# First block: selection rounds spread two to a projection tile and over the bias steps of attention units 0 to 19

## The chip, the cores and the metric

The kernel runs on one core of one Trainium2 chip. The metric is the device time of one execution in microseconds. Five engines work side by side, each with its own queue that is worked off strictly in order: PE (TensorE) multiplies, ACT (ScalarE) and DVE (VectorE) do elementwise work and empty PE's accumulators, POOL (GpSimd) adds a few tensors and issues DMAs, SP (SyncE) issues the weight loads. They meet only in semaphores: an instruction that finishes raises one, another engine's queue stands still until a count is reached.

## The reference, cut to what matters

Two model blocks run one after the other on 512 tokens of width 1024. The change lies in the first, which has two layers. Each layer is: SwiGLU feed-forward, RMS norm, one input projection to 2244 columns, three kinds of attention (8 heads with a sliding window, 4 heads in blocks, 4 heads with a learned selection of keys), output projection, SwiGLU again. The part that matters is the selection: for each query, the 128 best-scored keys are kept and all others are masked.

```python
dots = jnp.einsum('bqhd,bsd->bqhs', qi, k_idx).astype(jnp.float32) * (IDX_DIM ** -0.5)
score = jnp.einsum('bqhs,bqh->bqs', jax.nn.relu(dots), wi)
score = jnp.where((key_pos[None, :] <= tq[:, None])[None], score, -jnp.inf)
_, idx = lax.top_k(score, n_keep)        # n_keep = 512 // 4 = 128
...
s = jnp.einsum('bqhd,bqkd->bhqk', qc, k_sel).astype(jnp.float32) * scale + bias
```

The queries are handled in four blocks of 128. Block 0 has only 128 keys, so it needs no selection. Blocks 1, 2 and 3 have 256, 384 and 512 keys.

## The kernel before, in words

**Precision.** Each weight tile (128 x 1024) is split on its way: ACT copies `w_raw` into `w_hi` (line 167), DVE subtracts to get `w_lo` (line 174), and PE forms three products for each pair (lines 196 to 198). Three split tiles and three raw tiles are held at a time. ACT may split tile n + 3 only when PE has used tile n; DVE's `split_lo` of that tile waits for ACT's half.

**Projection (lines 1329 to 1352 for PE).** The 18 tiles of the input projection are worked in a fixed order. Tiles 0 to 3 give the selection's queries, its keys and the latent. Behind tile 3 PE forms the index scores and DVE adds them up in `work` (1152 columns: 256, 384 and 512 for the query blocks 1, 2, 3; the profile calls it `topk`). Tiles 4, 5 and 6 are the value trio: PE works them as one step, and only at its end are their three slots free. Tiles 7 to 17 are single again.

**Selection rounds (`topk_rounds`, from line 1147).** One call of `rounds(dve)` issues one round on DVE: `max` finds the eight largest values of each row (MAX8, line 1160), `match_replace` strikes them out (MATCH_VALUE_LOAD and MATCH_REPLACE8, line 1162). Sixteen rounds find 128 keys, so there are 48 rounds in a layer: 0 to 15 on 256 columns, 16 to 31 on 384, 32 to 47 on 512. The last round of each sixteen is followed by a comparison that turns the row into a mask (TENSOR_SCALAR, line 1166) and raises `sel_done`. In DVE's queue, four rounds stand behind the `split_lo` of each projection tile from tile 6 on. These are 12 tiles, so all 48 rounds stand in the queue before the attention starts; a loop behind the tiles issues whatever is left over, which is nothing.

**Attention (`Attention`, from line 521).** There are 64 units: four query blocks of 16 heads. Unit u is scored by PE (line 588), DVE adds the bias and takes the row maximum (`bias(u)`, line 720, the bias step), ACT takes the exponential (line 662), PE turns the probabilities (line 612), ACT or DVE copies them out (lines 689 and 764, DVE for odd units of the first block), PE multiplies by the values (line 627). DVE's queue holds, for each u: the copy of unit u if odd, then `bias(u + 2)`, then at the end of each eight units the division (lines 741 to 751). PE scores unit u + 2 only behind the turning of unit u. Before the first unit DVE clears `q_wide` (line 758), ACT fills it with the first queries (line 677), and only then can PE score unit 0. After each sixteen units the output of one query block is turned, the first time behind the turning of unit 17: PE line 597, ACT line 698, DVE line 775; ACT reaches that step behind the exponential of unit 19, and PE takes up unit 18 again when DVE is through with it. Before each bias step DVE calls `combined(eng, u)`, which for the selecting heads (units 28 to 31, 44 to 47 and 60 to 63) waits until POOL has added mask and bias.

Of the kernel before, what the change touches and what calls it, by code (L numbers as in the profile page):

```python
# [53 lines left out]
def program(nc, io):  # L54
# [11 lines left out]
    with top:  # L66
# [988 lines left out]
        def first_layers(ctx, shared, Hh, Hl, near, far, lv, upc, nsink, tri, QA, KD, VA, QB, KB, VB, QC, CKV, KCc, VC,  # L1055
# [43 lines left out]
            IDX_AFTER, CKV_AFTER, TRIO = 3, 8, 4  # L1099
# [47 lines left out]
            def topk_rounds():  # L1147

                state = {"n": 0, "sem": 3}

                def one(dve):
                    n = state["n"]
                    if n >= 3 * TOPK_ROUNDS:
                        return False
                    qb, r = n // TOPK_ROUNDS + 1, n % TOPK_ROUNDS
                    a, e = spans[qb]
                    dve.wait_ge(topk, state["sem"])
                    dve.max(best[:, :], work[:, a:e]).then_inc(topk, 1)  # L1160
                    dve.wait_ge(topk, state["sem"] + 1)
                    dve.match_replace(work[:, a:e], best[:, :], work[:, a:e], -3e38).then_inc(topk, 1)
                    state["sem"] += 2
                    if r == TOPK_ROUNDS - 1:
                        dve.wait_ge(topk, state["sem"])
                        dve.tensor_scalar(work[:, a:e], work[:, a:e], -2e38, BIG, ALU.is_gt, ALU.mult
                                          ).then_inc(sel_done, 1)
                    state["n"] += 1
                    return True

                return one
# [31 lines left out]
            with nc.Fori(0, DEPTH) as layer:  # L1203
                mlp_a.beside, mlp_b.beside = conditioning_beside(0, layer), conditioning_beside(1, layer)
                with nc.Block() as block:
                    @block.sync
                    def _(sp):
                        sp.dma_start(lv[:], io["layer_vecs"][bass.ds(layer, 1)].rearrange("a p n -> (a p) n")
                                     ).then_inc(vecs_in, 16)
                        st.load(sp, layer * LAYER1_TILES)  # L1210
# [156 lines left out]
                    def _(act):  # L1367
# [15 lines left out]
                        for j, (kind, dst) in enumerate(order):  # L1383
# [25 lines left out]
                            if j == IDX_AFTER:  # L1409
                                for i, (qb, _) in enumerate((q, i) for q in range(1, NQ) for i in range(4)):  # L1410
                                    nk = 128 * (qb + 1)
                                    act.wait_ge(idx_mm, i + 1)
                                    if i >= 2:
                                        act.wait_ge(acc_done, i - 1)
                                    act.activation(relu[:, i % 2, 0:nk], ps[:, 4 + i % 2, 0:nk], ACT.Relu, scale=1.0 / 16
                                                   ).then_inc(relu_done, 1)
# [20 lines left out]
                    @block.vector  # L1437
                    def _(dve):
                        st.start(st.split_lo, dve)
                        dve.wait_ge(vecs_in, 16)  # L1440
                        dve.tensor_scalar(nsink[:, :], lv[:, 25:33], -1.0, None, ALU.mult).then_inc(nsink_done, 1)
                        norms[0].vector(dve)
                        mlp_a.vector(dve)
                        dve.wait_ge(small, 64)
                        norms[1].vector(dve)
                        rounds = topk_rounds()
                        for j in range(N_IN1):
                            st.split_lo(dve, n_mix + j + st.n_hl)
                            if j == IDX_AFTER:

                                n = 0
                                for qb in range(1, NQ):
                                    a, e = spans[qb]
                                    for i in range(4):
                                        dve.wait_ge(relu_done, n + 1)
                                        w = WI[:, qb, i:i + 1]
                                        if i == 0:
                                            m = dve.tensor_scalar(work[:, a:e], relu[:, n % 2, 0:e - a], w, None, ALU.mult)
                                        else:
                                            dve.wait_ge(acc_done, n)  # L1460
                                            m = dve.scalar_tensor_tensor(out=work[:, a:e], in0=relu[:, n % 2, 0:e - a],
                                                                         scalar=w, in1=work[:, a:e], op0=ALU.mult,
                                                                         op1=ALU.add)
                                        m.then_inc(acc_done, 1)
                                        n += 1
                                    dve.wait_ge(acc_done, n)
                                    dve.tensor_tensor(work[:, e - 128:e], work[:, e - 128:e], tri[:, :], ALU.add
                                                      ).then_inc(topk, 1)
                            if j >= TRIO + 2:
                                for _ in range(4):  # L1470
                                    rounds(dve)
                            if j == CKV_AFTER + 1:
                                dve.wait_ge(ckv_inv, 1)
                                dve.scalar_tensor_tensor(out=CKV[:, :], in0=CKV[:, :], scalar=lv[:, 24:25], in1=relu[:, 0, :],
                                                         op0=ALU.mult, op1=ALU.mult).then_inc(ckv_n, 1)
                        while rounds(dve):
                            pass

                        def combined(eng, u):
                            if u == 0:  # L1480
                                eng.wait_ge(nsink_done, 1)
                            if u in comb_of:
                                eng.wait_ge(comb_done, comb_of[u] + 1)

                        att.vector(dve, combined)
                        proj.vector(dve)
                        norms[2].vector(dve)
                        mlp_b.vector(dve)
# [685 lines left out]
```

## Time and profile before

| | |
|---|---|
| median of 3 runs | 4356.09 us (4355.25 to 4361.63) |
| profiled execution | 4354.72 us, its span 4353.2 us |
| busy share PE, weight load, DVE, ACT | 91%, 74%, 52%, 36% |
| mean granted TensorE clock | 0.953 |

The span is what the profile covers; the execution's own time is 1.5 us more. The first block's layer 0 has its projection and attention between some 440 and 685 us, layer 1 the same about 1075.4 us later. Busy shares are means over the whole kernel. For this change the stretch between 500 and 612 us matters, and there the order of events on DVE, ACT and PE.

### The profile page before, as it was taken

How to read it: one execution, taken by the hardware profiler on the slowest of the kernel's cores; microseconds unless marked ns; L12 is line 12 of the kernel's file. 1: busy time of each engine (PE TensorE's matmuls, PEld its weight loads, DVE VectorE, ACT ScalarE, POOL GpSimd, SP SyncE). 2: the span in 40 equal slices, each digit the busy share in tenths (PEclk: the TensorE clock that was granted, in tenths of full speed). 3: DMA queues.
4: the chain of work that ended last, by engine and by line, in shares of the span. 5: the costliest groups of instructions: out<-in, count | busy, mean ns of one | idle time of the engine just before them, and what ended most of it. 6: DMA issues, size and time to landing. Idle time of an engine off the chain costs nothing. (4 is left out here: it accounts for less than half of the span.)

```text
span 4353.2 us, 52924 instructions
## 1 busy us (share of the span) xinstructions
PE 3941.1 (91%) x19258; PEld 3213.4 (74%) x19258; DVE 2270.2 (52%) x4044; ACT 1586.7 (36%) x2672; POOL 126.5 (3%) x188
## 2 busy tenths in 40 slices
PE   5999978999899997999969999699998679798999
PEld 3887766888688776688848887588887457576887
DVE  3665563666566666366632454355555344444555
ACT  2223353222322336322255454322221574743222
POOL 1000000000100000000000000000000000000000
PEclk9999989999999998999989999899999889899999
DMA  6443202443544220244211110121221110102332
GB/s 239 135 136 100 63 25 78 136 130 111 186 131 140 82 73 15 87 136 144 88 57 53 44 42 24 48 63 59 62 63 49 30 39 1 39 1 73 97 96 77
DMA packets 99854, 354.04 MB, mean 81 GB/s; under 512 B 11139, under 2 KB 14723, under 8 KB 98776
## 3 DMA queue, kind: packets, MB, share of 16 engines
q1 hardware_dynamic: 76632, 274.64, 20.8%
q0 software_dynamic: 18304, 70.33, 5.0%
q10 hardware_dynamic: 4736, 6.62, 0.4%
q8 instruction: 117, 1.92, 0.2%
q14 instruction: 65, 0.53, 0.0%
HBM read 345.73 MB, written 11.06 MB: 82 GB/s over the span
## 5 line engine op out<-in xcount | busy, mean ns | idle before, releaser
L167 ACT ACTIVATE w_hi<-w_raw 128x1024 fp32r<-128x1024 f32 x500 | 529.4, 1060 | 1902.5 <-PE ps L198 1733.9
L174 DVE TENSOR_TENSOR w_lo<-w_raw,w_hi 128x1024 fp32r<-128x1024 f32 x500 | 615.0, 1231 | 1161.2 <-ACT w_hi L167 1160.8
L196 PE MATMUL ps<-h_hi,w_hi 128*128 128x512 f32 (+1 forms) x2824 | 1094.2, 387 | 66.6 <-DVE h_lo L255 34.2
L197 PE MATMUL ps<-h_lo,w_hi 128*128 128x512 f32 (+1 forms) x2824 | 1083.3, 384 | 0.0
L198 PE MATMUL ps<-h_hi,w_lo 128*128 128x512 f32 (+1 forms) x2824 | 1082.1, 383 | 0.0
L196 PEld LDWEIGHTS ps<-h_hi,w_hi 128*128 128x128 f32 x2824 | 537.2, 190 | 192.3 <-issue 54.9
L198 PEld LDWEIGHTS ps<-h_hi,w_lo 128*128 128x128 f32 x2824 | 537.8, 190 | 103.9
L197 PEld LDWEIGHTS ps<-h_lo,w_hi 128*128 128x128 f32 x2824 | 538.8, 191 | 100.4 <-issue 1.4
L196 PE MATMUL ps<-a_hi,w_hi 128*128 128x512 f32 x1472 | 549.0, 373 | 3.3 <-DVE ctx_x L454 3.3
L197 PE MATMUL ps<-a_lo,w_hi 128*128 128x512 f32 x1472 | 546.8, 371 | 0.0
L198 PE MATMUL ps<-a_hi,w_lo 128*128 128x512 f32 x1472 | 546.0, 371 | 0.0
L196 PEld LDWEIGHTS ps<-a_hi,w_hi 128*128 128x128 f32 x1472 | 277.0, 188 | 57.2 <-DVE ctx_x L454 6.3
L198 PEld LDWEIGHTS ps<-a_hi,w_lo 128*128 128x128 f32 x1472 | 276.8, 188 | 49.1
L197 PEld LDWEIGHTS ps<-a_lo,w_hi 128*128 128x128 f32 x1472 | 277.1, 188 | 47.6
L454 DVE SCALAR_TENSOR_TENSOR x<-ps,x 128x512 f32<-128x512 f32 x352 | 231.5, 685 | 54.6 <-PE ps L198 52.6
L454 DVE SCALAR_TENSOR_TENSOR x<-ps,mod,x 128x512 f32<-128x512 f32 x256 | 188.0, 748 | 94.0 <-PE ps L198 94.0
L402 ACT ACTIVATE a_hi<-val 128x512 fp32r<-128x512 f32 (+1 forms) x184 | 106.0, 592 | 307.2 <-DVE val L438 307.2
L662 ACT ACTIVATE arena<-arena,nm 128x768 f32<-128x768 f32 (+3 forms) x160 | 130.9, 818 | 218.0 <-DVE nm L720 217.4
L240 PE MATMUL ps<-scratch,ones 128*128 128x512 f32 (+1 forms) x144 | 76.2, 682 | 98.8 <-ACT scratch L220 98.8
L612 PE MATMUL ps<-ident,arena 128*128 128x128 f32 x784 | 119.2, 284 | 31.7 <-DVE h_lo L775 26.4
L419 DVE TENSOR_TENSOR a_lo<-val,a_hi 128x512 fp32r<-128x512 f32 (+1 forms) x184 | 115.2, 640 | 62.5 <-ACT a_hi L402 62.5
L240 PEld LDWEIGHTS ps<-scratch,ones 128*128 128x128 f32 x144 | 27.3, 223 | 144.8 <-ACT scratch L220 124.2
(243 smaller groups left out, 4661.9 us busy)
## 6 DMA issues: line engine op xcount, KB each, us to landing
w_raw<-in_w_first SPq DMA_DIRECT2D x316, 512.0 KB, 3.6
w_raw<-in_w_mlp SPq DMA_DIRECT2D x128, 512.0 KB, 3.6
shared<-in_w_ada POOLq DMA_DIRECT2D x96, 512.0 KB, 4.3
w_raw<-in_w_odd SPq DMA_DIRECT2D x30, 512.0 KB, 3.6
w_raw<-in_w_even SPq DMA_DIRECT2D x26, 512.0 KB, 3.6
near_stage<-near_bias POOLq DMA_DIRECT2D x32, 256.0 KB, 2.9
bias_rows<-bias_line SPq DMA_DIRECT2D x1, 5120.0 KB
shared<-silu_cond POOLq DMA_DIRECT2D x4, 1024.0 KB, 4.9
```

What stands on the lines that cost most here:

```text
L167: act.activation(self.hi[:, n % H, :], self.raw[:, n % R, :], ACT.Copy).then_inc(self.hi_done, 1)
L174: dve.tensor_tensor(self.lo[:, n % self.n_hl, :], self.raw[:, n % self.n_raw, :], self.hi[:, n % self.n_hl, :].bitcast(F32), ALU.subtract) ...
L196: pe.matmul(out, lhs[0], rhs[0], start=start, stop=False)
L197: pe.matmul(out, lhs[0], rhs[1], start=False, stop=False)
L198: return pe.matmul(out, lhs[1], rhs[0], start=False, stop=stop)
L240: pe.matmul(self.acc(), ones[:, :], self.tmp["sq"][:, c % 2, 0:self.n], start=(c == 0), stop=(c == self.nk - 1)).then_inc(self.sum_done, 1)
L402: m = act.activation(self.hi[s][:, 2 * (c % 2) + j, :], self.val[s][:, j, :], ACT.Copy)
L419: m = dve.tensor_tensor(self.lo[s][:, a, :], self.val[s][:, j, :], self.hi[s][:, a, :].bitcast(F32), ALU.subtract)
L454: m = dve.scalar_tensor_tensor(out=stream["x"][:, o, :], in0=ps[:, self.down_bank(8 * c + o, s), 0:stream["n"]], scalar=self.gains(s, o), ...
L612: m = pe.transpose(ps[:, 4 + t % 2, 128 * j:128 * j + 128], tmp["s"][:, u % 2, 128 * (b + j):128 * (b + j) + 128], ident[:, :])
L662: act.activation(tmp["s"][:, u % 2, 0:n], tmp["s"][:, u % 2, 0:n], ACT.Exp, bias=tmp["nm"][:, u % 16:u % 16 + 1], scale=-1.0, accum_out=tm ...
```

## The change

DVE's queue now holds two rounds behind each projection tile from tile 4 (`TRIO`) on, in place of four from tile 6 on. The loop that issues what is left is gone. Instead `combined(eng, u)`, which DVE's queue passes before the bias step of each unit, issues one round as long as there are any. Fourteen tiles by two rounds are rounds 0 to 27; rounds 28 to 47 stand before the bias steps of units 0 to 19. No instruction is added or removed.

```diff
-                            if j >= TRIO + 2:
-                                for _ in range(4):
+                            if j >= TRIO:
+                                for _ in range(2):
                                     rounds(dve)
...
-                        while rounds(dve):
-                            pass
-
                         def combined(eng, u):
                             if u == 0:
                                 eng.wait_ge(nsink_done, 1)
+                            rounds(eng)
                             if u in comb_of:
                                 eng.wait_ge(comb_done, comb_of[u] + 1)
```

## Rows read from the trace of the kernel before

**Rows 1.** Busy time by stretch: PE, PEld, DVE, ACT, POOL; clock, DMA share, GB/s

```profile
500.00:563.50 63.50, 62.82 (x276) 51.12 (x276) 58.72 (x135) 24.22 (x33) 2.79 (x2) 1.00 0.33 100
563.50:579.60 16.10, 0.00 (x0) 0.01 (x1) 15.01 (x29) 1.80 (x4) 0.00 (x0) 0.64 0.22 65
579.60:600.00 20.40, 18.04 (x96) 14.63 (x97) 11.01 (x54) 16.88 (x68) 0.00 (x0) 0.87 0.01 2
```

**Rows 2.** Timeline of PE behind the projection (start us, us, ..., [idle before <-releaser])

```profile
579.63 1.19 PE L588 MATMUL ps<-shared,q_wide 128*128 128x128 f32 x4 [16.37 <-ACT q_wide L677]
```

**Rows 3.** Timeline of ACT at the projection's end, layer 0, then layer 1

```profile
563.35 1.06 ACT L167 ACTIVATE w_hi<-w_raw 128x1024 fp32r<-128x1024 f32 x1 [3.90 <-PE ps L198]
...
579.17 1.30 ACT L677 ACTIVATE q_wide<-shared 64x128 f32<-64x128 f32 x4 [14.28 <-DVE q_wide L758]
...
1638.74 1.06 ACT L167 ACTIVATE w_hi<-w_raw 128x1024 fp32r<-128x1024 f32 x1 [3.90 <-PE ps L198]
```

**Rows 4.** Timeline of DVE: one selection round on 384 columns to the next

```profile
525.88 0.55 DVE L1160 MAX8 best<-topk 128x8 f32<-128x384 f32 x1
...
527.11 0.56 DVE L1160 MAX8 best<-topk 128x8 f32<-128x384 f32 x1
```

**Rows 5.** Timeline of DVE: rounds on 512 columns and what follows them

```profile
549.40 0.36 DVE L1166 TENSOR_SCALAR topk<-topk 128x384 f32<-128x384 f32 x1
549.68 1.22 DVE L174 TENSOR_TENSOR w_lo<-w_raw,w_hi 128x1024 fp32r<-128x1024 f32 x1
550.82 0.69 DVE L1160 MAX8 best<-topk 128x8 f32<-128x512 f32 x1
...
551.62 0.68 DVE L1162 MATCH_REPLACE8 topk<-best,topk 128x512 f32<-128x512 f32 x1
552.33 0.69 DVE L1160 MAX8 best<-topk 128x8 f32<-128x512 f32 x1
...
556.17 0.68 DVE L1162 MATCH_REPLACE8 topk<-best,topk 128x512 f32<-128x512 f32 x1
556.76 1.22 DVE L174 TENSOR_TENSOR w_lo<-w_raw,w_hi 128x1024 fp32r<-128x1024 f32 x1
...
578.59 0.48 DVE L758 MEMSET q_wide<- 128x512 f32 x1
```

**Rows 6.** Timeline of DVE: bias steps of units 0, 1, 3; copy for unit 3

```profile
580.54 0.35 DVE L720 CUSTOM_DVE_ANT_0 scratch<-ps,bias_a,minus_sinks 128x128 f32<-128x128 f32 x1 [1.46 <-PE ps L588]
...
580.86 0.35 DVE L720 CUSTOM_DVE_ANT_0 scratch<-ps,bias_a,minus_sinks 128x128 f32<-128x128 f32 x1
...
583.06 0.35 DVE L720 CUSTOM_DVE_ANT_0 scratch<-ps,bias_a,minus_sinks 128x128 f32<-128x128 f32 x1
...
584.93 0.29 DVE L764 COPY scratch<-ps 128x128 f32<-128x128 f32 x1 [0.17 <-PE ps L612]
```

**Rows 7.** Timeline of DVE: bias steps of units 19, 20, 22, 24

```profile
599.82 0.47 DVE L720 CUSTOM_DVE_ANT_0 scratch<-ps,bias_a,minus_sinks 128x256 f32<-128x256 f32 x1
...
604.81 0.49 DVE L720 CUSTOM_DVE_ANT_0 scratch<-ps,bias_a,minus_sinks 128x256 f32<-128x256 f32 x1 [1.03 <-PE ps L588]
...
608.13 0.48 DVE L720 CUSTOM_DVE_ANT_0 scratch<-ps,bias_a,minus_sinks 128x256 f32<-128x256 f32 x1 [1.54 <-PE ps L588]
...
610.65 0.42 DVE L720 CUSTOM_DVE_ANT_0 scratch<-ps,bias_bc 128x256 f32<-128x256 f32 x1 [0.35 <-PE ps L588]
```

**Rows 8.** Timeline of DVE: zeroing and the step of unit 19 in layer 1

```profile
1653.97 0.48 DVE L758 MEMSET q_wide<- 128x512 f32 x1
...
1675.11 0.47 DVE L720 CUSTOM_DVE_ANT_0 scratch<-ps,bias_a,minus_sinks 128x256 f32<-128x256 f32 x1
```

**Rows 9.** Busy time by stretch: the granted clock behind unit 19

```profile
606.00:608.00 2.00, 2.00 (x11) 1.82 (x9) 0.49 (x2) 1.43 (x5) 0.00 (x0) 0.50 0.00 0
...
610.00:612.00 2.00, 2.00 (x15) 1.61 (x14) 1.17 (x7) 1.79 (x6) 0.00 (x0) 1.00 0.00 0
```

**Rows 10.** Waits between 480 and 780 us (total, times, longest)

```profile
DVE scratch L720 <- PE ps L588: 27.8, 39, 1.5
```

## The prediction

> **What bounds the kernel now.** I read the busy time by stretch first, then the timelines of PE, ACT and DVE where one stretch goes over into the next, then the waits.
>
> In the projection PE is the bound: it is busy for 62.82 of 63.5 us at full clock. DVE is nearly full as well, 58.72 us [rows 1]. The reader is to see what comes next: from 563.5 to 579.6 PE does nothing, while DVE works for 15.0 of 16.1 us [rows 1]. PE's timeline says 16.37 us idle, released by ACT's filling of `q_wide` [rows 2], and ACT had itself waited 14.28 us for DVE's zeroing of it [rows 3]. That zeroing stands in DVE's queue behind all 48 rounds, at 578.59 [rows 5]. So here the selection rounds set the end.
>
> Then units 0 to 19. Between 579.6 and 600.0 DVE is busy for 11.01 of 20.40 us, ACT for 16.88 [rows 1]. No engine is full. The units go round PE, DVE, ACT and PE, and DVE's waits are for PE's scores (27.8 us in 39 waits between 480 and 780 us [rows 10]). DVE has 9.4 us of gaps here.
>
> The change moves 20 rounds from a place where DVE alone sets the end into this second stretch. It is won if the gaps hold them. They don't.
>
> **The price of one round.** On 384 columns, MAX8 to the next MAX8 takes 527.11 - 525.88 = 1.23 us [rows 4]. On 512 columns it takes 552.33 - 550.82 = 1.51 us [rows 5]. Both include the wait of the next MAX8 for the replacement it reads. An instruction that doesn't read it starts sooner: the replacement at 551.62 is followed by a MAX8 0.71 us later, the one at 556.17 by a `w_lo` 0.59 us later [rows 5]. In the new order a bias step or a copy follows each round, neither of which reads `work`. I therefore take 1.23 - 0.12 = 1.11 and 1.51 - 0.12 = 1.39 us, and keep the full prices as the upper end. A comparison costs 549.68 - 549.40 = 0.28 us [rows 5], and must wait for its round, which then costs the full price.
>
> **Projection tiles 4 to 17.** Two rounds on 256 or 384 columns (at most 2.5 us) and a `w_lo` of 1.14 us (549.68 to 550.82 [rows 5]) make 3.6 us. PE's pace is 62.82 us for 11 tiles and a few small products, some 5.4 us a tile (x276 matmuls, 11 x 24 and 12 [rows 1]), so DVE stays ahead and PE waits for nothing new. Cost nothing. The rounds now put behind tiles 4 and 5 don't run under the value trio: each stands behind a `w_lo` whose `w_hi` needs the trio's slots. They run right behind the trio, ahead of the `w_lo` of tiles 8 and 9. The one for tile 8 comes 2 us later than now, with 5.4 us in hand.
>
> **The start of the attention, removed.** Tile 17 has two rounds behind it, numbers 26 and 27. They stand behind a `w_lo` whose `w_hi` ACT begins at 563.35, when PE has used tile 17, and needs 1.06 us for, to 564.41 [rows 3]. DVE: 564.45, plus 1.14 for `w_lo`, plus 1.23 + 1.11 for the rounds, is 567.93. There the zeroing starts. It started at 578.59 [rows 5]: 10.7 us sooner. In layer 1, ACT's start is at 1638.74 [rows 3] and the zeroing at 1653.97 [rows 8], which gives 10.65. Of PE's 16.4 us some 5.7 stay.
>
> **Units 0 to 19, added.** I sum DVE's work from the start of the zeroing to the start of unit 19's bias step, because with it DVE has no gap left. Before, this took 599.82 - 578.59 = 21.23 us [rows 5, 7], in layer 1 21.14 [rows 8].
> - Old work: zeroing 0.48, and 11.01 less the 0.18 that lies behind 599.82: 11.31.
> - Rounds 28 to 31: 4 x 1.11 = 4.44. Rounds 32 to 47: 16 x 1.39 = 22.24.
> - Two of them are followed by a comparison: 2 x (0.12 + 0.28) = 0.80.
> - Idle before unit 0: its bias step follows the start of the zeroing by 580.54 - 578.59 = 1.95 us [rows 5, 6], since ACT and PE come between. Zeroing and round 28 fill 1.59 of it: 0.36.
>
> The sum is 39.15 us, 17.9 more than now. Is it DVE at every unit? Two bias steps now lie at least 2 x 1.39 plus their own 2 x 0.3 apart, 3.4 us. PE and ACT need for the same way 3.32 us at their slowest, on 256 keys and at the low clock (unit 20 to 22: 608.13 - 604.81 [rows 7]; clock 0.50 [rows 9]); on 128 keys it is less. The copy for unit 3 came 584.93 - 583.06 = 1.87 us behind its bias step [rows 6]; the new order has 0.32 + 1.39 + 0.3 = 2.0 us there. So DVE sets it, if narrowly in places.
>
> **Behind unit 19.** ACT's exponential of unit 19, the turn (602.11) and unit 20 (604.81) hang on unit 19's bias step [rows 7], and are carried along. Nothing queued behind DVE has slack to give: PE's next score waits for the bias step two units earlier. POOL's additions need the first mask only at unit 28 and the last at unit 60; all are early enough. The weight tiles for the output projection are split before unit 0, as now. Net: 17.9 - 10.7 = 7.2 us a layer.
>
> **TensorE's clock.** Before, the clock is at 0.50 of full (1.2 GHz) between 606 and 608, behind the pause of the turn, and back at 1.00 from 610 [rows 9]. In the new order PE is idle for about half of each unit, so it will mostly be at the lower level before the turn as well, where DVE covers it. Then unit 20 starts at the lower level from its first instruction. I add 0.3 us a layer for that, nearly the price of one unit at the lower level instead of the higher (0.4, rival 2); the ends are 0 and 2.4 (six units).
>
> The Trainium skill ("TensorE: Matmul & The Clock Gate", section "Why this matters for your kernels") says that idle gaps between bursts of matmuls put the engine back to half rate. By that rule the trace agrees: 0.50 behind the turn [rows 9]. Taken as a rule for all of the sparse units and what follows them, it is the second rival.
>
> **Sum.** 7.2 + 0.3 = 7.5 us a layer, 15.0 for two. On the profiled execution, 4354.72 us with a span of 4353.2, that is 4369.7. The median of the runs lies 1.4 us above it, so the forecast is **4371 us**, slower by 0.35%. Ends a layer: if each bias step overlaps a further 0.08 us of the MAX8 behind it (as `w_lo`, 1.22 us long, is followed after 1.14 [rows 5]), 5.6; if no round overlaps its successor, 7.2 + 18 x 0.12 = 9.4, plus 2.4 for the clock, 11.8. That is 4367 to 4380.
>
> **Rivals.**
> 1. *The gaps hold the rounds (faster).* The rounds run while DVE waits for scores, units keep their pace, and only the earlier start is left: -10.7 x 2, 4334.7 us. For it: DVE is idle 46% of the stretch. It decides from the point where 20 rounds fit in the gaps. They are 27.5 us, the gaps 9.4 [rows 1], and a round of 1.39 us is longer than the single gaps (1.46 before unit 0 [rows 6] is the longest of the bias steps). Chance 0.04. The Trainium skill ("Perfetto Trace Analysis", section "Optimization Strategy") says that performance may be improved by interleaving stretches that have different bounds; taken alone it speaks for this rival. The rows say that DVE was already interleaved with PE in the projection (58.72 of 63.5 us), and that the change leaves some 1.8 of 5.4 us a tile idle there.
> 2. *The clock stays low behind unit 19.* Two units take 3.32 us at 0.50 and 2.52 at the higher level (unit 22 to 24 [rows 7]), 0.4 us a unit. If units 20 to 31 all run low, 12 x 0.4 = 4.8 us a layer, 4381 us. Against it: from unit 20 on PE's work is as dense as before, and there the clock was back at 1.00 from 610 on [rows 9]. Chance 0.09.
> 3. *The delay is given back later.* DVE's waits for scores behind unit 19 could shrink. Then the time is that of before, 4356 us. Against it: these waits are a ring through PE and ACT, started by unit 19 itself. Chance 0.05.
>
> My own case has 0.82.
>
> **How the numbers follow.** Some 0.2% (9 us) is what a measurement of this kernel can tell from no change. Slower by more: most of my case, 0.80, and rival 2: 0.89. Within: rival 3 and the low edge of my case: 0.07. Faster: 0.04. The range of 8 in 10 takes my case's ends, the spread of the medians, and half of rival 2: 4363 to 4381.
>
> **What would show it.** In the new profile, layer 0: the zeroing at about 568 and PE's idle time before unit 0 near 6 us; DVE busy for over 95% between there and unit 19's bias step, with MAX8 to bias step 1.4 us; that bias step at 607 (now 599.82); unit 20 behind it by 5.0 to 5.3 us; all later events 7 to 8 us later. Wrong if bias steps wait for PE's scores between units 4 and 19 (then PE or ACT sets the pace, and more time is lost), if PE waits for `w_lo` in tiles 8 to 17, or if the distance from unit 19 to the output projection changes.

## The result, and the profile after

The changed kernel takes 4367.49 us (median of 17 runs, 4356.48 to 4375.97), the kernel before 4355.81 us (17 runs, 4346.47 to 4366.00). The ratio is 1.0028, with a 95% interval of 1.0019 to 1.0036: slower by 12 us (8 to 16). The forecast was 4371 us, slower by 15, with a range of 4363 to 4381. The profiled execution took 4370.76 us with a span of 4369.2.

The rows that answer to those of before, by stretch (columns as in [rows 1]). The two stretches are the projection, and the way from the zeroing to unit 19's bias step:

```profile
500.00:563.50 63.50, 62.29 (x275) 50.64 (x273) 40.25 (x91) 24.22 (x33) 1.43 (x2) 1.00 0.37 108
567.10:604.50 37.40, 29.57 (x104) 23.51 (x104) 36.20 (x116) 17.79 (x69) 0.00 (x0) 0.51 0.02 8
```

DVE, busy for 58.72 us in the projection before, is now busy for 40.25, and PE works on as it did. Behind it DVE is busy for 36.20 of 37.40 us, where it was for 11.01 of 20.40 [rows 1]. So 18.5 us of DVE's work left a stretch in which PE set the pace and the rounds cost nothing, and went into one in which DVE sets it. Of the 20 rounds that moved, only the last 8 had run behind PE's last tile, where they were in the way. In the second stretch PE is busy for 29.57 of 37.4 us, at a mean clock of 0.51, and is held back by DVE.

PE, then ACT, behind the projection ([rows 2, 3] answer):

```profile
568.16 1.20 PE L588 MATMUL ps<-shared,q_wide 128*128 128x128 f32 x4 [5.88 <-ACT q_wide L677]
...
562.38 1.06 ACT L167 ACTIVATE w_hi<-w_raw 128x1024 fp32r<-128x1024 f32 x1 [3.90 <-PE ps L198]
...
567.71 1.31 ACT L677 ACTIVATE q_wide<-shared 64x128 f32<-64x128 f32 x4 [3.79 <-DVE q_wide L758]
...
1644.31 1.06 ACT L167 ACTIVATE w_hi<-w_raw 128x1024 fp32r<-128x1024 f32 x1 [3.90 <-PE ps L198]
```

PE's idle time went from 16.37 to 5.88 us: the gain.

DVE, from the zeroing on ([rows 5 to 8] answer). Rounds on 384 columns, then rounds on 512, with the bias step or copy that follows; the turn; layer 1:

```profile
567.13 0.48 DVE L758 MEMSET q_wide<- 128x512 f32 x1
567.53 0.50 DVE L1160 MAX8 best<-topk 128x8 f32<-128x384 f32 x1
...
568.97 0.35 DVE L720 CUSTOM_DVE_ANT_0 scratch<-ps,bias_a,minus_sinks 128x128 f32<-128x128 f32 x1 [0.28 <-PE ps L588]
569.25 0.08 DVE L720 DVE_READ_ACCUMULATOR2_ANT nm<- 128x1 f32 x1
569.25 0.56 DVE L1160 MAX8 best<-topk 128x8 f32<-128x384 f32 x1
...
570.37 0.34 DVE L720 CUSTOM_DVE_ANT_0 scratch<-ps,bias_a,minus_sinks 128x128 f32<-128x128 f32 x1
...
574.03 0.69 DVE L1160 MAX8 best<-topk 128x8 f32<-128x512 f32 x1
...
575.42 0.34 DVE L720 CUSTOM_DVE_ANT_0 scratch<-ps,bias_a,minus_sinks 128x128 f32<-128x128 f32 x1
575.69 0.08 DVE L720 DVE_READ_ACCUMULATOR2_ANT nm<- 128x1 f32 x1
575.69 0.29 DVE L764 COPY scratch<-ps 128x128 f32<-128x128 f32 x1
575.89 0.68 DVE L1160 MAX8 best<-topk 128x8 f32<-128x512 f32 x1
...
577.28 0.34 DVE L720 CUSTOM_DVE_ANT_0 scratch<-ps,bias_a,minus_sinks 128x128 f32<-128x128 f32 x1
...
602.33 0.41 DVE L764 COPY scratch<-ps 128x256 f32<-128x256 f32 x1
...
604.51 0.48 DVE L720 CUSTOM_DVE_ANT_0 scratch<-ps,bias_a,minus_sinks 128x256 f32<-128x256 f32 x1
...
606.80 1.68 DVE L775 TENSOR_TENSOR h_lo<-ps,h_hi 128x128 fp32r<-128x128 f32 x8 [1.81 <-ACT h_hi L698]
610.18 0.48 DVE L720 CUSTOM_DVE_ANT_0 scratch<-ps,bias_a,minus_sinks 128x256 f32<-128x256 f32 x1 [1.70 <-PE ps L588]
...
616.45 0.42 DVE L720 CUSTOM_DVE_ANT_0 scratch<-ps,bias_bc 128x256 f32<-128x256 f32 x1 [0.36 <-PE ps L588]
...
1649.05 0.48 DVE L758 MEMSET q_wide<- 128x512 f32 x1
...
1686.42 0.48 DVE L720 CUSTOM_DVE_ANT_0 scratch<-ps,bias_a,minus_sinks 128x256 f32<-128x256 f32 x1
...
1698.42 0.42 DVE L720 CUSTOM_DVE_ANT_0 scratch<-ps,bias_bc 128x256 f32<-128x256 f32 x1 [0.35 <-PE ps L588]
```

The reader is to see that after 568.97 no row has idle time in brackets until 606.80. From there to unit 19 DVE never waits for another engine: bias step to bias step is 1.40 us with a round on 384 columns (568.97 to 570.37) and 1.86 with one on 512 and a copy (575.42 to 577.28), where it was 1.0 on the mean before (580.54 to 599.82 for units 0 to 19 [rows 6, 7]). That is the loss: unit 19's bias step comes 37.4 us behind the zeroing, not 21.2.

### The profile page after: what moved, and what is told of

It reads as the page before. It is cut to its first block and busy times, and to the rows that moved or that the text cites. A ratio compares the mean times of both kernels' runs of the same rounds, so it can differ in the third digit from the quotient of the medians.

```text
span 4369.2 us, 52924 instructions
## 1 busy us (share of the span) xinstructions
PE 3968.1 (91%) x19258; PEld 3235.0 (74%) x19258; DVE 2263.0 (52%) x4044; ACT 1588.6 (36%) x2672; POOL 123.9 (3%) x188
```

## The experiments

Each was profiled; where a ratio stands, it is to the kernel before on the same chip. "Way A" is from the start of ACT's last `w_hi` of the projection to unit 19's bias step, "way B" from there to unit 24's. Before, they were 36.5 and 36.4 us, and 10.8 and 10.8 (layers 0 and 1) [rows 3, 7, 8]; changed, 42.1 and 42.1, and 11.9 and 12.0.

**The tiles' part alone.** Against the kernel before, whose loop behind tile 17 stays and now issues the last 20 rounds:

```diff
-                            if j >= TRIO + 2:
-                                for _ in range(4):
+                            if j >= TRIO:
+                                for _ in range(2):
                                     rounds(dve)
```

> One part of the change alone: two rounds per tile from the value trio on, but the last 20 rounds stand as one block behind tile 17, ahead of the zeroing of q_wide, and none at the bias steps. My account (DVE's queue alone sets the pace, and the gaps between bias steps take a third of the 20 rounds): the zeroing in layer 0 at 567.1 + 4 x 1.25 + 16 x 1.51 + 0.5 = 596.8 us, unit 19's bias step 21.2 us behind it at 618 (604.5 in the changed kernel, 599.8 before). Some 12.4 us a layer over the changed kernel, 18 over the kernel before: about 4392 us. Rival (the rounds hurt because they stand inside the ring of PE, ACT and DVE and lengthen it): with the ring free of them the time comes out at or below the changed kernel's 4367.

Measured: 4395.66 us, ratio 1.0085 (1.0070 to 1.0101), 37 us over the kernel before. DVE in this kernel:

```profile
598.98 0.48 DVE L758 MEMSET q_wide<- 128x512 f32 x1
...
620.20 0.47 DVE L720 CUSTOM_DVE_ANT_0 scratch<-ps,bias_a,minus_sinks 128x256 f32<-128x256 f32 x1
```

The zeroing comes 34.7 us behind the last `w_hi` (564.24), unit 19 follows it by 21.2 as before. So the gaps between the bias steps did hold part of what they were given: with the 20 rounds as one block, way A is 56.0 us, with the rounds spread over the units 42.1. The rival falls. Interleaving is worth 13.9 us a layer against the block. But in the kernel before only 8 of these 20 rounds were left behind the last tile; the other 12 ran beside PE's projection and cost nothing.

**Four per tile, twenty at the units.**

```diff
-                            if j >= TRIO:
-                                for _ in range(2):
+                            if TRIO + 2 <= j < TRIO + 9:
+                                for _ in range(4):
                                     rounds(dve)
```

> The units' part as in the changed kernel (rounds 28 to 47 at units 0 to 19), but the 28 rounds of the tiles are packed four to a tile on tiles 6 to 12, so none stands behind tile 17. My account: only the start changes. Behind tile 17 DVE has w_lo alone, so the zeroing comes 2.5 us sooner than in the changed kernel, at about 564.7 to 565.6 in layer 0, and everything behind it up to the end is 2.4 to 2.5 us a layer sooner: 4367.5 - 5 = 4362.5 us, still slower than before by some 7. Rival (how the rounds are spread over the tiles is what costs or helps, for instance by PE waiting for w_lo): PE shows new waits in tiles 8 to 12 and the 5 us are not seen.

Measured: ratio 1.0008 (0.9999 to 1.0018), against 1.0028 for the change.

```profile
565.54 0.48 DVE L758 MEMSET q_wide<- 128x512 f32 x1
...
602.60 0.48 DVE L720 CUSTOM_DVE_ANT_0 scratch<-ps,bias_a,minus_sinks 128x256 f32<-128x256 f32 x1
```

The zeroing stands 2.37 us behind the last `w_hi` (563.17), where it is 4.75 in the changed kernel, and way A is 39.4 in both layers: 2.7 us less, against 2.4 expected. PE shows no wait for `w_lo` in tiles 8 to 17, and from the first `w_hi` behind the trio to the last one it is 65.28 us in this run, in the changed kernel and in the one before. How the 28 rounds are spread over the tiles is of no account, except that two behind tile 17 stand on the path: 5 us of the 12 lost, by the timeline (the two intervals all but meet).

**Three per tile, six at the units.**

```diff
-                                for _ in range(2):
+                                for _ in range(3):
```

> The changed kernel with three rounds behind each tile from the value trio on, so that 42 stand in the tiles and only 6 at the units, 0 to 5. A test of the sum at another dose. My account: the zeroing of q_wide now has three rounds on 512 columns behind tile 17, 1.14 + 3 x 1.51 = 5.7 us behind ACT's w_hi, and DVE is up to 0.7 us late by then: some 570.5 in layer 0 where the last w_hi starts at 563.3. Units 0 to 5 then take 10.6 us from the zeroing to unit 5's bias step where the kernel before takes 6.7 (five steps of 1.39 + 0.3, three copies of 0.2, unit 0 hidden): 3.9 more. From unit 6 on the old pace. Net -8.0 + 3.9 = -4.1 us a layer under the kernel before, plus up to 1.1 for the clock behind the turn: ratio 0.998 to 0.9986, about 4348 to 4350 us where the kernel before has 4356. Rival (any round at a bias step costs the units more than DVE's own time): slower than before.

Measured: 4347.48 us against 4355.57, ratio 0.9982 (0.9972 to 0.9993): faster by 8 us.

```profile
569.60 0.48 DVE L758 MEMSET q_wide<- 128x512 f32 x1
...
580.61 0.34 DVE L720 CUSTOM_DVE_ANT_0 scratch<-ps,bias_a,minus_sinks 128x128 f32<-128x128 f32 x1
...
595.79 0.47 DVE L720 CUSTOM_DVE_ANT_0 scratch<-ps,bias_a,minus_sinks 128x256 f32<-128x256 f32 x1
```

Zeroing 7.05 us behind the last `w_hi` (7.2 expected), unit 5 at 11.0 behind that (10.6 expected), then 15.2 to unit 19, where it was 14.6 before. In that last stretch the mean clock is 0.78, and was 1.00 before; that this is what costs the 0.6 us isn't shown. Ways A and B together are 3.2 and 3.1 us shorter than before, 3.0 to 4.1 expected. The sum holds at another dose, and with the sign changed: the same change with a 3 for a 2 is a gain.

**PE's idle time in the units filled.**

```diff
+                    if self.fill and 1 <= u <= self.fill:
+                        pe.matmul(ps[:, 1, 0:256], ident[:, :], X[:, 0, 0:256], start=True, stop=True)
...
+            att.fill = 17
```

> The changed kernel, with one more matmul on PE (identity by 256 columns of x, into an accumulator bank that nothing reads) behind each of units 1 to 17 of the first block, so that PE's idle time in the units with rounds is filled. The result is unchanged. My account: the clock in units 0 to 19 covers nothing that counts, since DVE sets the pace there. Unit 19's bias step stays within 0.5 us of 604.5; if the clock goes up to 1.00 before the turn, the way from unit 19's bias step to unit 24's, 11.9 us in the changed kernel and 10.8 before, shrinks to about 10.8: 1.1 us a layer, 2.2 in all, 4365 us. If the clock stays at 0.50 in spite of the fill, nothing changes or it is slower by a few us. Rival (the low clock is the main cost of the change): with the clock up, unit 19's bias step comes several us sooner and the kernel comes to 4356 to 4360 us.

Measured: ratio 1.0030 (1.0019 to 1.0040), no different from the change. The clock from unit 6 to unit 10, first of the changed kernel, then of this one:

```profile
578.00:588.00 10.00, 8.13 (x30) 6.53 (x30) 9.73 (x33) 5.08 (x22) 0.00 (x0) 0.50 0.01 2
```

```profile
578.00:588.00 10.00, 8.45 (x41) 5.21 (x40) 9.72 (x33) 5.24 (x22) 0.00 (x0) 1.00 0.01 2
```

The clock went from 0.50 to 1.00 there (1.2 to 2.4 GHz), and DVE's order in time is the same to a hundredth: zeroing to unit 19's bias step 37.39 us, 37.38 in the changed kernel. So the low clock inside the units costs nothing. But way B stayed at 12.0: half of my expectation was wrong. PE's pause at the turn was 4.71 us, with the clock at 1.00 before it, and still PE took up unit 18 at the lower one (its two transposes take 0.66 us at the lower level and 0.41 at the higher):

```profile
608.79 0.66 PE L613 MATMUL ps<-ident,scratch 128*128 128x128 f32 x2 [4.71 <-DVE h_lo L778]
```

**The turn filled too.** On top of the last:

```diff
                         turn(self.turn_at[u - 1])
+                        if self.fill and u - 1 < 20:
+                            for _ in range(4):
+                                pe.matmul(ps[:, 1, :], ident[:, :], X[:, 0, :], start=True, stop=True)
```

> The changed kernel with PE's idle time filled as in the run with one more matmul behind each unit, and with four more matmuls (identity by 512 columns of x, some 0.86 us each, result unread) on PE behind the first turn of each layer, so that PE's pause between the turn's transposes and its next unit, 4.1 us in the changed kernel, 4.7 with the fill and 2.9 before, becomes one of some 1 us. The result is unchanged. My account: the pause is what puts PE at the lower clock when it takes up unit 18 again. Then the first transposes behind the turn take 0.41 us in place of 0.66, and the way from unit 19's bias step to unit 24's is 10.8 us in both layers in place of 12.0; unit 19's bias step itself stays 42.1 us behind the last w_hi. Ratio to the kernel before some 1.0025. Rival (the lower clock behind the turn has another cause, or is chance): 0.66 us and 12.0 us in one layer or both.

Measured: ratio 1.0023 (1.0009 to 1.0037). PE at the turn, in the changed kernel and in this one:

```profile
602.84 1.66 PE L597 MATMUL ps<-ident,scratch 128*128 128x128 f32 x8
...
608.62 0.66 PE L612 MATMUL ps<-ident,scratch 128*128 128x128 f32 x2 [4.12 <-DVE h_lo L775]
```

```profile
604.25 0.41 PE L613 MATMUL ps<-ident,scratch 128*128 128x128 f32 x2 [1.28 <-DVE h_lo L781]
```

Way A is 42.1 in both layers. The first transposes take 0.41 us in place of 0.66, and way B is 9.5 us in both layers, 2.4 less than changed and 1.3 less than before: more than expected, because the clock is now at 1.00 all the way (600.1 to 609.7). So with the units filled, PE's pause at the turn is what makes way B long. The 5 us of two layers don't show in the time: the ratio can't be told from the change's 1.0028.

In the changed kernel itself the clock shows the same, by stretch (columns as in [rows 1]), inside the pause:

```profile
604.50:607.50 3.00, 0.00 (x1) 0.00 (x0) 1.19 (x7) 2.37 (x11) 0.00 (x0) 1.00 0.00 0
607.50:608.60 1.10, 0.00 (x0) 0.01 (x1) 0.98 (x5) 0.00 (x0) 0.00 (x0) 0.50 0.00 0
```

After 37 us mostly at 0.50 it stands at 1.00 when PE stops, and falls to 0.50 while PE stands still, before unit 18. No run fills the turn and leaves the units sparse; that this alone would do is not shown.

**Both kernels profiled once more.**

> The kernel before, profiled once more: how much do the two numbers that I compare move by themselves? The start of the last w_hi of the projection in layer 0 was 563.35 before, 562.38 in the changed kernel and 562.5 to 564.2 in the runs derived from it. The way from unit 19's bias step to unit 24's was 10.83 and 10.83 before, 11.94 and 12.00 changed. If the clock's phase is by chance, one of the two layers may now show 11.5 to 12; if the sparse units cause it, both stay at 10.8.

> The changed kernel, profiled once more. From the last w_hi of the projection to unit 19's bias step 42.1 us in both layers, since DVE alone sets it (within 0.2). The way from unit 19's bias step to unit 24's again 11.9 to 12.0 in both layers if PE's longer pause at the turn makes it, 10.8 in one of them if it is chance.

Measured: 4350.03 us for the kernel before and 4370.71 for the changed one, one execution each. DVE of the kernel before, layer 1, and its PE behind the turn:

```profile
1672.34 0.47 DVE L720 CUSTOM_DVE_ANT_0 scratch<-ps,bias_a,minus_sinks 128x256 f32<-128x256 f32 x1
...
1684.61 0.42 DVE L720 CUSTOM_DVE_ANT_0 scratch<-ps,bias_bc 128x256 f32<-128x256 f32 x1 [0.36 <-PE ps L588]
...
1676.46 0.66 PE L612 MATMUL ps<-ident,scratch 128*128 128x128 f32 x2 [2.86 <-DVE h_lo L775]
```

Way B was 10.85 us in layer 0 and 12.27 in layer 1; the changed kernel had 11.97 and 12.20. Way A of the changed kernel was 42.1 in both layers again. That of the kernel before was 36.85 and 37.42, where the first profile had 36.47 and 36.37: without the rounds DVE doesn't set the pace alone, and the way is not fixed. So the change costs 6.4 and 4.6 us a layer between these two profiles, 6.8 and 6.9 between the first two. The last `w_hi` of layer 0 started at 562.52 and 562.68, so the 0.97 us between the first two profiles there is scatter. Counting the first turn of each layer in all profiles here without added matmuls on PE: where the pause is 2.86 us, PE's first two transposes take 0.41 us seven times and 0.66 five times; where it is 3.85 us or more (this order of rounds, and the run with four per tile), 0.66 in all six. Way B is 10.8 to 10.9 us in the seven, 11.1 to 12.3 in the five and 11.65 to 12.2 in the six. The change makes way B surely long, where it was so by chance; on the mean of the four layers of each kernel that is 12.0 against 11.2 us.

**All rounds in the projection.** DVE has 17.2 us of nothing to do under the value trio, in the kernel before:

```profile
499.15 1.23 DVE L174 TENSOR_TENSOR w_lo<-w_raw,w_hi 128x1024 fp32r<-128x1024 f32 x1 [17.24 <-ACT w_hi L167]
```

```diff
                         for j in range(N_IN1):
+                            if j == TRIO:
+                                for _ in range(TOPK_ROUNDS):
+                                    rounds(dve)
                             st.split_lo(dve, n_mix + j + st.n_hl)
...
-                            if j >= TRIO:
-                                for _ in range(2):
+                            if TRIO <= j < N_IN1 - 1:
+                                for _ in range(3 if j < 10 else 2):
                                     rounds(dve)
...
-                            rounds(eng)
```

> All 48 rounds inside the projection: the 16 rounds on 256 columns stand ahead of the w_lo of tile 7, so that DVE does them while PE works the value trio and DVE has 17.2 us of nothing to do; then three rounds behind each of tiles 4 to 9, two behind tiles 10 to 16, none behind tile 17 and none at the units. My account: 16 rounds of 0.98 us are 15.7 us and end before the trio does; the rest costs at most 3 x 1.51 + 1.14 = 5.7 us of DVE against PE's 5.4 a tile, mostly 4.2 to 4.9. So the zeroing comes at 564.5 + 1.1 = 565.6 in layer 0 (578.6 before, 567.1 changed) and the units run at their old pace, unit 19's bias step at 586.8. 13 us a layer under the kernel before: 4330 us. Rival (DVE beside the trio slows PE or ACT, or w_lo comes late for tiles 8 to 10): PE waits for w_lo, and less than half of the 26 us is seen.

Measured: 4333.43 us against 4358.6, ratio 0.9944 (0.9931 to 0.9958). By stretch (the trio, then tiles 7 to 17), and DVE:

```profile
482.00:500.00 18.00, 15.68 (x90) 15.36 (x88) 15.68 (x50) 3.88 (x10) 1.40 (x2) 0.99 0.00 1
500.00:563.50 63.50, 62.63 (x275) 51.05 (x276) 55.91 (x111) 23.78 (x32) 0.00 (x0) 1.00 0.36 105
```

```profile
566.37 0.48 DVE L758 MEMSET q_wide<- 128x512 f32 x1
568.10 0.35 DVE L720 CUSTOM_DVE_ANT_0 scratch<-ps,bias_a,minus_sinks 128x128 f32<-128x128 f32 x1 [1.25 <-PE ps L588]
...
588.31 0.47 DVE L720 CUSTOM_DVE_ANT_0 scratch<-ps,bias_a,minus_sinks 128x256 f32<-128x256 f32 x1
```

DVE was busy for 15.68 us under the trio, and PE shows no new wait for `w_lo`: it is busy for 62.63 of the next 63.5 us. The zeroing stands 2.4 us behind the last `w_hi` (15.2 before). By the ratio the gain was 24 us of 26 expected. Ways A and B together are 10.9 and 11.5 us shorter than before, 13 expected a layer; 1.2 of what is missing is way B, 12.0 in both layers. One cost was not expected: from the first `w_hi` behind the trio to the last it is 66.22 and 66.57 us in place of 65.28. In both layers PE waits here for DVE, which has rounds on 512 columns ahead of the latent's last step, `ckv`, before which PE can't start L1298:

```profile
529.24 1.12 PE L1298 MATMUL ps<-ckv,w_kv_up 128*128 128x512 f32 x2 [0.53 <-DVE ckv L1477]
```

In layer 0 PE takes 2.68 us from its last product ahead of L1298 to the next tile's first, in place of 1.90. So the rounds are not quite free there: 0.9 and 1.3 us.

**The zeroing ahead of the sixteen.**

```diff
                             if j == TRIO:
+                                dve.memset(q_wide[:, :, :], 0.0).then_inc(att.q_zero, 1)
```

> All 48 rounds in the projection as in the run that puts sixteen under the value trio, and the zeroing of q_wide moved ahead of those sixteen, so that ACT can fill q_wide as soon as it has emptied tile 17. My account: 0.48 us more under the trio, which fits barely or delays w_lo of tile 7 by nothing (1.2 us of room). ACT's filling of q_wide starts 1.2 us sooner (at 565.6 where the last w_hi starts at 564.0) and unit 0 with it: 1.2 us a layer, 2.4 in all, ratio to the kernel before 0.9938 where the other has 0.9944, about 4331 us. That is less than five rounds can tell; the timeline decides. Rival (ACT or the turn holds unit 0): no sooner than 4.1 us behind ACT's last w_hi.

Measured: 4326.65 us against 4355.57, ratio 0.9931 (0.9917 to 0.9945). ACT at the projection's end:

```profile
563.89 1.06 ACT L167 ACTIVATE w_hi<-w_raw 128x1024 fp32r<-128x1024 f32 x1 [3.90 <-PE ps L198]
564.85 0.58 ACT L1403 ACTIVATE shared<-ps 128x512 f32<-128x512 f32 x1
565.46 1.30 ACT L678 ACTIVATE q_wide<-shared 64x128 f32<-64x128 f32 x4
```

ACT goes from emptying tile 17 to `q_wide` with no wait. Unit 0's bias step follows the last `w_hi` by 2.6 us (4.1 in the run above, 17.2 before). 1.5 us in layer 0 and 1.7 in layer 1, 1.2 expected; the ratios alone can't tell the two runs apart.

**The same, with three turns filled.** Two matmuls of 512 columns on PE behind the turns at units 17, 33 and 49, nothing in the units.

```diff
                         turn(self.turn_at[u - 1])
+                        if self.fill and u < len(units):
+                            for _ in range(2):
+                                pe.matmul(ps[:, 1, :], ident[:, :], X[:, 0, :], start=True, stop=True)
```

> The version with all rounds in the projection and the early zeroing, and two matmuls more (identity by 512 columns of x, result unread) on PE behind the turns of units 17, 33 and 49 in each layer of the first block, so that PE's pause of 2.9 us at each turn becomes one of some 1.2 us. The result is unchanged. My account: PE takes up the next unit at the higher clock and keeps it, as in the run with the filled turn, where the way from unit 19's bias step to unit 24's fell to 9.5 us (10.8 to 12.0 without). That is 1.3 to 2.5 us a turn, six turns, 8 to 15 us: ratio to the kernel before 0.990 to 0.9915, about 4315 us. Rival (the gain in that run needs the longer fill or the filled units): 10.8 us or more at the turns, ratio 0.993 as without the fill.

Measured: 4317.99 us against 4360.31, ratio 0.9913 (0.9900 to 0.9927): the fastest of all. PE's pause is 1.15 us in place of 2.86 and its first transposes take 0.41 us at all six turns, where the run above had 0.66 at four of the six. Way B is 9.5 us in both layers (10.85 and 11.08 above). From turn to turn it takes PE 23.17 and 25.84 us in layer 0, in place of 24.65 and 27.37, and 23.16 and 25.83 in layer 1, in place of 24.71 and 28.38.

```profile
586.85 1.88 PE L647 MATMUL ps<-x,ident 128*128 128x512 f32 x4
589.88 0.41 PE L613 MATMUL ps<-ident,scratch 128*128 128x128 f32 x2 [1.15 <-DVE h_lo L780]
```

The intervals of this run and the one above overlap, so it is the timeline, 1.3 to 2.6 us for each of six turns, and not the ratios that shows what the fill is worth.

## Why the prediction was right

By its own steps, in us, for layer 0 and layer 1, from the first profile of each kernel:

| step | forecast | measured |
|---|---|---|
| last `w_hi` to zeroing | 4.58 | 4.75, 4.74 |
| zeroing to unit 19's bias step | 39.15 | 37.38, 37.37 |
| the 20 rounds and 2 comparisons in it | 27.48 | 27.6 |
| the rest of DVE's work in it, idle time included | 11.67 | 9.8 |
| unit 19 to unit 24 | 10.8 + 0.3 | 11.94, 12.00 |
| net over before, a layer | 7.5 | 6.8, 6.9 |

- *Projection at no cost.* Right: 65.28 us from the trio's end to the last `w_hi` before and after. The run with four per tile shows that PE is indifferent to how these 28 rounds lie there.
- *The start.* Right to 0.2 us. 5.88 us of PE's idle time stayed, 5.7 forecast, and the run with four per tile takes the two rounds of tile 17 out of it.
- *The price of a round.* Right. 574.03 to 575.42 is the 1.39 us that came of taking 0.12 off for a successor that doesn't read the row.
- *DVE at every unit.* Right, with not one wait for another engine between units 1 and 19, though the pace of PE was near.
- *The old work.* 1.8 us too much, and this is the term that was mis-sized. I took DVE's busy time as it was with gaps between its instructions. Packed, they overlap: the read of the accumulator behind each bias step (83 ns) begins together with the MAX8 or copy behind it (at 569.25 and 575.69), so that 19 reads take 0.11 us of DVE's time in place of 1.5. The nine copies and the zeroing, whose successors start 0.08 to 0.09 us before their ends, make up part of the rest. I had named an overlap of this size as my lower end, 5.6 us a layer, instead of taking it.
- *The clock.* The sign was right, the size too small: 1.1 to 1.2 us a layer between the first profiles, not 0.3, and 0.8 on the mean of both profiles of each kernel. The cause that I gave, sparse units before the turn, is not what the runs point to. With the units filled and the clock at 1.00 it was as much; with the pause at the turn filled too it was gone. Nor is PE idle for half of each unit, as I wrote: it is busy for 29.57 of 37.40 us, at the lower clock. PE at the turn, before:

```profile
600.00 1.06 PE L597 MATMUL ps<-ident,scratch 128*128 128x128 f32 x8 [0.56 <-DVE scratch L764]
603.93 0.41 PE L612 MATMUL ps<-ident,scratch 128*128 128x128 f32 x2 [2.86 <-DVE h_lo L775]
```

In both kernels PE takes up unit 18 again 4.11 us behind the start of unit 19's bias step. The pause is longer because PE's transposes of the turn (L597) are done sooner against that step: they wait for the copy of unit 17. It began 0.33 us ahead of the bias step before (599.49), and now begins 2.18 us ahead (602.33), with a whole round and a comparison between. Everything else at the turn waits for the bias step.
- *Rivals.* The gaps hold the rounds: no (I had also called a round of 1.39 us longer than any single gap, which the 1.46 us before unit 0 is not); the gain of 10.5 us from the earlier start is there, and the units took it and more. Low clock up to unit 31: no; from unit 24 on the distance to before stays at 5.80 us in layer 0 (616.45 to 610.65, the same at the output projection, 690.96 to 685.16). Given back later: no, by the same rows.

Of the 16.0 us between the two profiled executions these steps make 13.7. The others are -1.0 before the projection's end in layer 0, -0.2 between the layers and 3.5 behind unit 24 of layer 1, where no instruction was changed. Left behind that unit are 2667.3 and 2663.8 us in the two profiles of the kernel before and 2670.8 and 2670.6 in those of the changed one; in the runs where nothing behind it differs it is 2664.0 to 2673.5, with and without rounds at the units, so these 3.5 us are taken as scatter. The medians' 12 us lie near the steps' 13.7. That the forecast of 15 came so near is in part luck: 1.8 us a layer too much of old work and some 0.8 too little for the clock partly cancelled.

## What to carry to other kernels

When work is moved from one engine's idle place to another, compare what it would fill with how full the other engines are there. Here the rounds cost nothing beside a PE that set the pace, and more than half of their own length between units that no engine fills (27.6 us of rounds lengthened the way by 16.2); the room was under the value trio, in front of an instruction that waited. Then count the queue of the engine that has become the bound, instruction by instruction, without the gaps: here it came within 5% (39.15 against 37.38 us), and it told that a smaller dose would be a gain.

## What the runs showed of the hardware

PE's clock, at 2.4 GHz before a pause of 2.86 us at a layer's first turn, was at that level again when PE came back in seven cases and at 1.2 GHz in five, with the same kernel giving both. Over all 56 pauses of 2.86 us in the twelve profiles PE came back at 2.4 GHz in 39. Coming back at 2.4 GHz is not the end of it: in the kernel before PE did so at 603.93, and the clock was at 0.50 from 606 to 608 all the same [rows 9]. Behind pauses of 3.85 to 4.72 us PE came back at 1.2 GHz in all eight cases, and behind pauses of 1.15 to 1.28 us at 2.4 GHz in all eight. Two matmuls that nobody reads, put into a pause, were worth 1.3 us and more to the units behind it. The Trainium skill ("TensorE: Matmul & The Clock Gate", section "Why this matters for your kernels") says to avoid idle gaps between bursts; the trace agrees, and adds that behind gaps of 2.86 us the level is a matter of chance. On DVE, the read of an accumulator (83 ns) costs next to nothing if an instruction without a wait follows it: it and the MAX8 behind it both begin at 569.25.
